# Six plain chunks instead of eight ahead of the pair runs of two feed-forward layers, with token-side sums in two bank sets and the plain chunks evacuated by ScalarE

## The chip, the cores and the metric

One core of a Trainium2 chip runs the whole model block. The metric is device time in microseconds, from three runs of the kernel before. TensorE multiplies, VectorE and GpSimd do elementwise work, ScalarE copies, squares and applies functions, SyncE issues the loads of the weights. SBUF holds 128 partitions; PSUM has eight banks of 128 x 512 floats, into which TensorE writes.

## The reference

Two transformer blocks over 512 tokens of width 1024. The change concerns the feed-forward layer of each, the first projection above all:

```
h = rms_norm(x, norm2_g[l])
f = jnp.square(jax.nn.relu(jnp.einsum('bsd,df->bsf', h, w_ff1[l])))
x = x + jnp.einsum('bsf,fd->bsd', f, w_ff2[l])
```

The second block has the same with `w_up`, `w_down` and `g_pre_mlp`. Width 1024 goes to 4096 and back. Ahead of the feed-forward layer stand, in block one, a gated unit with a convolution, and in block two, two kinds of attention.

## The kernel before, in words

All weights come as one stream of chunks of 128 x 1024, 512 KB each, into four slots. Each float is split into a high part (rounded to the 32-bit form that TensorE takes at full rate) and a low part (the rest), and each product is three: high times high, high times low, low times high. GpSimd splits the weights (`split_chunk`: one copy, `high`, and one subtraction, `low`, L564 and L567); ScalarE and VectorE split the activations (`xh`, `xl`). A chunk of the first projection gives one tile of 128 features x 512 tokens, by 8 x 3 = 24 products over 512 columns.

The feed-forward layer's hidden width of 32 tiles is done in two halves of 16 (`FH`). In each half the first projection is followed by the second one ("down"). The first half has `PLAIN` = 8 plain chunks and then a run of pairs; the other half is a run of eight pairs. **A pair** computes two tiles (2 x 2 blocks: two halves of the tokens, two halves of the features) by seven block products instead of eight, in the manner of Strassen and Winograd. Each block product is 12 products over 256 columns (`product`), so a pair has 84 of them, where two plain chunks have 48 over 512 columns. The seven need sums on both sides:

- Token side, once per layer: four sums of x blocks for each of four rounds k (`scaled_parts`, `t_sums`, `t_round`). ScalarE scales two parts into banks 4 and 5, VectorE makes four sums there (L2326), ScalarE rounds them into `t_high`, VectorE makes the low parts `t_low` (L2331).
- Weight side, once per pair: four sums of the raw weights in banks 6 and 7 by VectorE (`weight_sums_first` L2360 and L2362, `weight_sums_last` L2368 and L2369), rounded by ScalarE (`sum_round`, L1683), low parts by VectorE (`weight_rest`, L2377).

VectorE adds the seven products up: `first_corner` (L2385) adds the second to the first, and must be done before the seventh may be written, since they share a bank; `second_product`, `fifth_product` and so on follow. A finished tile goes through relu, square (`uh`, high) and low part (`rest_of_tile`, L2422).

The plain chunks of a layer feed TensorE while the token-side sums and the first pair's weight sums are made. Three of them run together while x is still being finished (`feed_first`, `several`); the others follow one by one, in banks `c % 4`. Behind the first products of the sixth chunk stand four turns (transposes) of the norm's summed squares (`norm_sums`), in bank 7 (`NB`). Tiles 0 to 3 are evacuated (relu, out of PSUM) by VectorE between the rounds of token sums, tiles 4 to 7 by ScalarE.

The order on each engine is that in which the code of its block is written; engines wait for each other by counting semaphores. The functions that the change touches are `plain_tiles` (ScalarE), `plain_run` and `t_sums` (VectorE), `feed_first` and `pair` (TensorE), `split_pair` (GpSimd). The projections, the attention and the second halves are not touched.

## Time and profile before

| | us |
|---|---|
| runs of before | 1082.06, 1082.08, 1083.15 (median 1082.08) |
| profiled execution | 1081.88 |
| its span | 1080.2 |
| TensorE busy | 1064.1, 99% of the span |
| VectorE busy | 701.3, 65% |
| GpSimd busy | 673.6, 62% |
| ScalarE busy | 400.7, 37% |
| end of the plain chunks, pairs: first layer | 193.1, 230.6 |
| end of the plain chunks, pairs: second layer | 791.85, 830.7 |

Busy time of TensorE is modelled: neighbouring products overlap in the pipeline, so how fast it goes is read from the starts. In the rows, a time in us from the span's start, a duration, the engine, the line, the operation and its operands stand in this order; [16.44 <-PE bank L766] is idle time just before and what ended it.

### The profile page before, as it was taken

What the parts mean: (1) busy time and instruction counts of PE and PEld (TensorE: products, weight loads), DVE (VectorE), ACT (ScalarE), POOL (GpSimd) and SP (SyncE); (2) the same over time, 40 slices, a digit from 0 to 9 for tenths busy, and PEclk for the clock granted to TensorE, in tenths of its full rate; (3) what the DMA queues carried; (4) which work ended last, traced back from release to release, by engine and by line L of the source; (5) the groups of instructions that cost most, each with busy time, mean ns of one, the idle gap of its engine ahead of it and who ended that gap; (6) DMA issues with size and microseconds to landing.
All of it is one profiled execution on the core that took longest, in us unless ns stands there. A gap on an engine that the chain in (4) does not pass through costs nothing.

```text
span 1080.2 us, 17261 instructions
## 1 busy us (share of the span) xinstructions
PE 1064.1 (99%) x6163; PEld 931.6 (86%) x6163; DVE 701.3 (65%) x1381; ACT 400.7 (37%) x817; POOL 673.6 (62%) x460
## 2 busy tenths in 40 slices
PE   9999999999999999999999999999999999999997
PEld 6878888998899988889788787777899888999886
DVE  5999778961158854548689878676888113886033
ACT  5156565540015541220202346655665000465012
POOL 7979857577636676667556433135856763557762
PEclk9999999999999999999999999999999999999999
DMA  7422223243213343334443232112223932234412
GB/s 262 137 91 66 61 96 98 80 155 117 97 59 118 111 156 104 100 110 142 117 133 102 90 86 60 40 60 78 61 96 134 198 98 66 92 118 173 179 59 78
DMA packets 52251, 115.54 MB, mean 107 GB/s; under 512 B 21840, under 2 KB 22480, under 8 KB 52176
## 3 DMA queue, kind: packets, MB, share of 16 engines
q1 hardware_dynamic: 31200, 105.40, 30.2%
q10 hardware_dynamic: 20976, 9.15, 3.4%
q8 instruction: 46, 0.75, 0.3%
q14 instruction: 29, 0.24, 0.1%
HBM read 105.09 MB, written 4.19 MB: 101 GB/s over the span
## 4 chain that ended last, share of the span: by engine, by line
PE 81%; DVE 11%; ACT 3%; issue 2%; POOL 2%; DMA 1%; SPq 0%; DVEq 0%; ACTq 0%; POOLq 0%
PE bank L766 80%; DVE bank L2118 5%; PE bank L1296 1%; POOL wl L567 1%; DVE tmp L2010 1%; ACT wh L1683 1%; DMA x<-xT 1%; DVE wl L2377 0%; DVE bank L2010 0%; POOL wh L564 0%; DVE gpad L2010 0%; DVE bank L2360 0%; PE bank L910 0%; ACT uh L1699 0%; DVE x L2191 0%
## 5 line engine op out<-in xcount | busy, mean ns | idle before, releaser
L567 POOL TENSOR_TENSOR wl<-raw,wh 128x1024 fp32r<-128x1024 f32 x140 | 334.2, 2387 | 11.7
L564 POOL TENSOR_SCALAR wh<-raw 128x1024 fp32r<-128x1024 f32 x139 | 149.2, 1073 | 231.7 <-PE bank L766 177.3
L766 PE MATMUL bank<-xh,wh 128*128 128x512 f32 (+2 forms) x747 | 256.4, 344 | 2.4 <-ACT vg L1577 1.5
L766 PE MATMUL bank<-xh,wl 128*128 128x512 f32 (+2 forms) x747 | 248.4, 336 | 0.0
L766 PE MATMUL bank<-xl,wh 128*128 128x512 f32 (+2 forms) x744 | 246.2, 338 | 0.8 <-DVE xl L2029 0.8
L766 PEld LDWEIGHTS bank<-xh,wh 128*128 128x128 f32 x747 | 141.9, 190 | 33.2 <-issue 19.5
L766 PEld LDWEIGHTS bank<-xl,wh 128*128 128x128 f32 x744 | 140.9, 190 | 14.2 <-DVE xl L2029 4.0
L766 PEld LDWEIGHTS bank<-xh,wl 128*128 128x128 f32 x747 | 142.0, 190 | 11.1
L1683 ACT ACTIVATE wh<-bank 128x512 fp32r<-128x512 f32 x96 | 52.2, 596 | 241.8 <-DVE bank L2362 103.1
L766 PE MATMUL bank<-uh,wh 128*128 128x512 f32 x320 | 123.2, 385 | 1.8 <-DVE ss L2412 0.9
L766 PE MATMUL bank<-uh,wl 128*128 128x512 f32 x320 | 121.3, 379 | 0.0
L766 PE MATMUL bank<-ul,wh 128*128 128x512 f32 x320 | 117.4, 379 | 0.0
L766 PE MATMUL bank<-t_high,wh 128*128 128x256 f32 x384 | 107.1, 279 | 0.3 <-DVE sq L2418 0.2
L766 PE MATMUL bank<-t_low,wh 128*128 128x256 f32 x384 | 105.6, 275 | 0.0
L766 PE MATMUL bank<-t_high,wl 128*128 128x256 f32 x384 | 105.6, 275 | 0.0
L766 PE MATMUL bank<-wh,uh 128*128 128x512 f32 x256 | 97.1, 379 | 0.4 <-POOL wl L567 0.4
L766 PE MATMUL bank<-wl,uh 128*128 128x512 f32 x256 | 97.0, 379 | 0.0
L766 PE MATMUL bank<-wh,ul 128*128 128x512 f32 x256 | 97.0, 379 | 0.0
L2377 DVE TENSOR_TENSOR wl<-bank,wh 128x512 fp32r<-128x512 f32 x96 | 63.2, 682 | 24.4 <-ACT wh L1683 24.1
L2010 DVE TENSOR_TENSOR bank<-bank,rb 128x512 f32<-128x512 f32 x16 | 11.2, 700 | 100.8 <-PE bank L766 100.8
L701 POOL TENSOR_SCALAR wh<-raw 128x512 fp32r<-128x512 f32 x24 | 15.0, 623 | 98.8 <-PE bank L766 98.8
L766 PEld LDWEIGHTS bank<-t_high,wh 128*128 128x128 f32 x384 | 73.6, 192 | 1.6 <-issue 0.6
(338 smaller groups left out, 2104.8 us busy)
## 6 DMA issues: line engine op xcount, KB each, us to landing
raw<-wstream SPq DMA_DIRECT2D x188, 512.0 KB, 3.5
x<-xT SPq DMA_DIRECT2D x8, 256.0 KB, 4.8
x4rows<-x_rows ACTq DMA_DIRECT2D x4, 512.0 KB, 7.5
out<-x4rows SPq DMA_DIRECT2D x8, 256.0 KB, 2.1
qd<-ropey ACTq DMA_DIRECT2D x16, 64.0 KB, 2.1
kd<-ropey ACTq DMA_DIRECT2D x16, 64.0 KB, 2.1
qa<-ropey SPq DMA_DIRECT2D x16, 64.0 KB, 2.0
ka<-ropey SPq DMA_DIRECT2D x16, 64.0 KB, 2.0
```

The lines of the kernel that those rows point to most:

```text
L564: nc.gpsimd.tensor_scalar(wh[c][:], raw[c][:], 1.0, 1.0, ALU.mult, ALU.mult).then_inc(high_ready, 1)
L567: nc.gpsimd.tensor_tensor(wl[c][:], raw[c][:], wh[c][:].bitcast(F32), ALU.subtract).then_inc(split_ready, 1)
L701: nc.gpsimd.tensor_scalar(high_b[:, 0:512], b[:, 512:], 1.0, 1.0, ALU.mult, ALU.mult).then_inc(high_ready, 1)
L766: return nc.tensor.matmul(out, stationary, moved, start=start, stop=stop)
L1296: last = nc.tensor.transpose(out[:, j * P:j * P + P], probs[2 * (n % 3) + e][:, j * P:j * P + P], ident[:])
L1683: A(wh[slot_of(p, role)][:, 512 * part:512 * part + 512], bank[7 - made % 2][:], ACT.Copy).then_inc(sum_rounded, 1)
L2010: return V.tensor_tensor(out, p, q, ALU.mult)
L2118: ins = V.scalar_tensor_tensor(out=out, in0=src, scalar=w, in1=acc, op0=ALU.mult, op1=ALU.add)
L2377: V.tensor_tensor(wl[slot][:, at], bank[7 - made % 2][:], wh[slot][:, at].bitcast(F32), ALU.subtract).then_inc(sum_ready, 1)
```

## The change

`PLAIN` goes from 8 to 6, so each layer has one pair more (five instead of four) behind its plain chunks. What makes room for that:

- The token sums of round k use banks 4 and 5 or banks 6 and 7 in turn (`t_banks`), and high and low parts of two sums lie in one tensor (`t_sides`), so that one operation over 512 columns rounds two sums, and one makes two low parts.
- All plain tiles are evacuated by ScalarE; VectorE has no evacuation left there.
- The turned squares go to bank 5 in the first layer and stay in bank 7 in the second (`norm_bank`), and wait for the token sums that used the bank.
- The first pair's slots, product banks and waits are numbered so that what follows stays as it was (`slot_of`, `free_at`, `FIRST_BANK`).
- On VectorE, the four small operations on the norm's rows stand behind the second layer's run of pairs instead of ahead of it.

```
-PLAIN = 8
+PLAIN = 6
...
+FIRST_BANK = (3, 0, 3, 1)
...
-    return (PAIR_RUNS[run_of(p)][0] + role) % SLOTS
+    first, _, count = PAIR_RUNS[run_of(p)]
+    return (first + 2 * count + role) % SLOTS
+
+
+def free_at(p, role):
+
+    first = PAIR_RUNS[run_of(p)][0]
+    return first - SLOTS + (slot_of(p, role) - first) % SLOTS + 1
...
+        t_sides = [at("t_sides0", [P, 2, 2, 4, Q], F32R, behind), at("t_sides1", [P, 2, 2, 4, Q], F32R, tmp_at)]
+        t_high = [t_sides[i // 2][:, i % 2, 0] for i in range(4)]
+        t_low = [t_sides[i // 2][:, i % 2, 1] for i in range(4)]
...
+        t_banks = [(bank[4], bank[5]), (bank[6], bank[7])] * 2 + [(bank[6], bank[7]), (bank[4], bank[5])] * 2
...
-            return bank[(7 * place_in(p) + i + run_of(p) // 3) % 5][:, EARLY]
+            return bank[(7 * place_in(p) + i + FIRST_BANK[run_of(p)]) % 5][:, EARLY]
+
+        def norm_bank(i):
+            return bank[5 if i == 5 else 7]
...
-                    pool.wait_ge(chunk_done, n - 3)
+                    pool.wait_ge(chunk_done, free_at(p, 0))
...
+                pe.wait_ge(t_ready, 14 if i == 13 else 6)
+                norm_sums(i, ss, 0, sq_added, squares)
...
-                    hooks = {0: lambda: norm_sums(i, ss, 0, sq_added, squares)} if c == 5 else {}
+                    hooks = {0: lambda: feed_norm(i, squares)} if c == PLAIN - 1 else {}
...
-                    pe.wait_ge(evacuated, e - 3)
+                    pe.wait_ge(evacuated, e - 2)
...
-                    pe.wait_ge(evacuated, e - 2)
+                    if run in (0, 2):
+                        pe.wait_ge(t_ready, 16 if run else 6)
...
-                    pe.wait_ge(t_ready, 32 if run else 16)
+                    pe.wait_ge(t_ready, 16 if run else 8)
...
+                if k % 4 >= 2:
+                    act.wait_ge(t_ready, 2 * k - 2)
+                for b, part, columns in zip(t_banks[k], (k % 4, 4 + k % 4), (EARLY, LATE)):
+                    A(b[:, EARLY], x[:, part, columns], ACT.Copy, scale=col(gain, part)).then_inc(scaled_part, 1)
...
-                for t, src in enumerate((bank[4][:, EARLY], bank[4][:, LATE], bank[5][:, EARLY], bank[5][:, LATE])):
-                    A(t_high[t][:, k % 4], src, ACT.Copy).then_inc(t_rounded, 1)
+                for sides, b in zip(t_sides, t_banks[k]):
+                    A(sides[:, :, 0, k % 4], two(b[:]), ACT.Copy).then_inc(t_rounded, 1)
...
+                def evacuate(c):
+                    act.wait_ge(chunk_done, c0 + c + 1)
+                    act.wait_ge(ul_ready, first + c - 1) if c >= 2 else act.wait_ge(sq_added, 6 * KT if first else 2 * KT)
+                    A(two(sq[c % 2][:]), by_token(bank[c % 4][:]), ACT.Relu).then_inc(evacuated, 1)
+
+                def squared(c):
                     act.wait_ge(evacuated, evacuations(first + c) + 1)
                     A(uh[:, c], sq[c % 2][:], ACT.Square).then_inc(uh_ready, 1)
                     A(sq[c % 2][:], sq[c % 2][:], ACT.Square).then_inc(square_ready, 1)
-                    if c < 3:
-                        scaled_parts(k0 + c + 1, gain)
-                    if c == PLAIN - 3:
-                        norm_sd(norm)
-                        sum_round(p, 0)
-                        sum_round(p, 1)
-                    if c == PLAIN - 2:
-                        sum_round(p, 2)
-                        sum_round(p, 3)
+
+                scaled_parts(k0, gain)
+                if first:
+                    act.wait_ge(xl_ready, 5 * KT)
+                else:
+                    act.wait_ge(xl_ready, 2 * KT)
+                    act.wait_ge(sq_added, 2 * KT)
+                scaled_parts(k0 + 1, gain)
+                t_round(k0)
+                evacuate(0)
+                t_round(k0 + 1)
+                scaled_parts(k0 + 2, gain)
+                squared(0)
+                evacuate(1)
+                scaled_parts(k0 + 3, gain)
+                t_round(k0 + 2)
+                squared(1)
+                evacuate(2)
+                t_round(k0 + 3)
+                squared(2)
+                evacuate(3)
+                squared(3)
+                evacuate(4)
+                squared(4)
+                norm_sd(norm)
+                sum_round(p, 0)
+                sum_round(p, 1)
+                evacuate(5)
+                squared(5)
+                sum_round(p, 2)
+                sum_round(p, 3)
...
+                def t_rest(i):
+                    dve.wait_ge(t_rounded, 2 * k + i + 1)
+                    sides = t_sides[i]
+                    V.tensor_tensor(sides[:, :, 1, k % 4], two(t_banks[k][i][:]),
+                                    sides[:, :, 0, k % 4].bitcast(F32), ALU.subtract).then_inc(t_ready, 1)
...
-                for c in range(4):
-                    t_sums(k0 + c, 0, gain)
-                    if c == 0:
-                        dve.wait_ge(sq_added, (6 if norm == 13 else 2) * KT)
-                    evacuate(c)
-                    t_sums(k0 + c, 1, gain)
-                    if c < 3:
-                        rest(c)
+                t_sums(k0, 0, gain)
+                t_sums(k0 + 1, 0, gain)
+                t_sums(k0, 1, gain)
+                t_sums(k0 + 1, 1, gain)
+                t_sums(k0 + 2, 0, gain)
+                rest(0)
+                t_sums(k0 + 2, 1, gain)
+                t_sums(k0 + 3, 0, gain)
+                rest(1)
+                t_sums(k0 + 3, 1, gain)
+                rest(2)
+                norm_total(norm)
+                dve.wait_ge(t_ready, 2 * k0 + 8)
+                weight_sums_first(p)
                 rest(3)
-                rest(4)
-                norm_total(norm)
-                weight_sums_first(p)
-                rest(5)
                 weight_rest(p, 0)
                 weight_rest(p, 1)
+                weight_sums_last(p)
+                rest(4)
                 norm_factor(norm)
-                weight_sums_last(p)
-                rest(6)
                 weight_rest(p, 2)
                 weight_rest(p, 3)
-                rest(7)
+                rest(5)
...
+            pair_run(2)
             dve.wait_ge(rn_ready, 14)
             link(mul(row_scale[:], rn[:, 0:TB], rn[:, 0:TB]))
             link(mul(row_weight[:], row_scale[:], row_scale[:]))
             link(V.reciprocal(row_weight[:], row_weight[:]))
             V.tensor_scalar(row_weight_mean[:], row_weight[:], 1.0 / D, None, ALU.mult).then_inc(row_scaled, 1)
-            pair_run(2)
```

Two places show what moves. ScalarE, first layer, from the rounding of the second round of token sums on; before (sq_75 and sq_76 are the two buffers of tiles, t_high_139 to 142 the high parts of the four token sums):

```order
L1673 ACTIVATE t_high_139<-bank 128x256
L1673 ACTIVATE t_high_140<-bank 128x256
L1673 ACTIVATE t_high_141<-bank 128x256
L1673 ACTIVATE t_high_142<-bank 128x256
L1717 ACTIVATE uh<-sq_76 128x512
L1718 ACTIVATE sq_76<-sq_76 128x512
L1664 ACTIVATE bank<-x,cols 128x256
L1666 ACTIVATE bank<-x,cols 128x256
```

and now, from the same point (t_sides_139 and 140 hold two sums each; L1727 is the evacuation):

```order
L1688 ACTIVATE t_sides_139<-bank 128x2x256
L1688 ACTIVATE t_sides_140<-bank 128x2x256
L1682 ACTIVATE bank<-x,cols 128x256 x2
L1731 ACTIVATE uh<-sq_75 128x512
L1732 ACTIVATE sq_75<-sq_75 128x512
L1727 ACTIVATE sq_76<-bank 128x512
L1682 ACTIVATE bank<-x,cols 128x256 x2
L1688 ACTIVATE t_sides_139<-bank 128x2x256
L1688 ACTIVATE t_sides_140<-bank 128x2x256
L1731 ACTIVATE uh<-sq_76 128x512
L1732 ACTIVATE sq_76<-sq_76 128x512
```

ScalarE has two evacuations between the rounds, and each rounding is two operations instead of four. VectorE, first layer, from the last addition to the sum of squares on; before (L2326 are the token sums, L2436 the evacuation, L2331 the low parts of the sums, L2422 that of a tile):

```order
L2309 TENSOR_TENSOR ss<-sq_76,bank 128x512
L2326 SCALAR_TENSOR_TENSOR bank<-x,cols,bank 128x256 x4
L2436 TENSOR_SCALAR sq_75<-bank 128x512
L2331 TENSOR_TENSOR t_low_143<-bank,t_high_139 128x256
L2331 TENSOR_TENSOR t_low_144<-bank,t_high_140 128x256
L2331 TENSOR_TENSOR t_low_145<-bank,t_high_141 128x256
L2331 TENSOR_TENSOR t_low_146<-bank,t_high_142 128x256
L2422 TENSOR_TENSOR ul<-sq_75,uh 128x512
L2326 SCALAR_TENSOR_TENSOR bank<-x,cols,bank 128x256 x4
```

and now:

```order
L2362 SCALAR_TENSOR_TENSOR bank<-x,cols,bank 128x256 x8
L2368 TENSOR_TENSOR t_sides_139<-bank,t_sides_139 128x2x256
L2368 TENSOR_TENSOR t_sides_140<-bank,t_sides_140 128x2x256
L2368 TENSOR_TENSOR t_sides_139<-bank,t_sides_139 128x2x256
L2368 TENSOR_TENSOR t_sides_140<-bank,t_sides_140 128x2x256
L2362 SCALAR_TENSOR_TENSOR bank<-x,cols,bank 128x256 x4
L2457 TENSOR_TENSOR ul<-sq_75,uh 128x512
L2368 TENSOR_TENSOR t_sides_139<-bank,t_sides_139 128x2x256
L2368 TENSOR_TENSOR t_sides_140<-bank,t_sides_140 128x2x256
L2362 SCALAR_TENSOR_TENSOR bank<-x,cols,bank 128x256 x4
```

VectorE makes the sums of two rounds at once, and has no evacuation; the low parts are two operations a round. From the norm's totals on (the first pair's weight sums, three low parts of tiles and the weight sums' low parts) its order is that of before, with tiles 3, 4 and 5 in the place of 5, 6 and 7; only the reciprocal of the norm stands two sums and a low part later.

## Rows read from the trace of the kernel before

**Rows 1.** The page, part 1: busy time, share, instructions.

```profile
PE 1064.1 (99%) x6163; PEld 931.6 (86%) x6163; DVE 701.3 (65%) x1381; ACT 400.7 (37%) x817; POOL 673.6 (62%) x460
```

**Rows 2.** TensorE in order of time, first layer.

```profile
166.78 0.38 PE L766 MATMUL bank<-xh,wh 128*128 128x512 f32 x1
...
177.57 0.38 PE L766 MATMUL bank<-xh,wl 128*128 128x512 f32 x1
...
178.15 0.46 PE L766 MATMUL bank<-xh,wh 128*128 128x512 f32 x1
...
193.12 0.27 PE L766 MATMUL bank<-xh,wh 128*128 128x256 f32 x1
...
230.53 0.28 PE L766 MATMUL bank<-t_high,wl 128*128 128x256 f32 x1
```

**Rows 3.** TensorE in order of time, second layer.

```profile
765.51 0.38 PE L766 MATMUL bank<-xh,wh 128*128 128x512 f32 x1
...
791.85 0.27 PE L766 MATMUL bank<-xh,wh 128*128 128x256 f32 x1
...
799.78 0.28 PE L766 MATMUL bank<-xh,wl 128*128 128x256 f32 x1
...
800.09 0.35 PE L766 MATMUL bank<-t_high,wh 128*128 128x256 f32 x1
...
801.75 0.35 PE L766 MATMUL bank<-xh,wh 128*128 128x256 f32 x1
...
830.63 0.28 PE L766 MATMUL bank<-t_high,wl 128*128 128x256 f32 x1
```

**Rows 4.** VectorE in order of time, the first addition of a pair.

```profile
197.63 0.41 DVE L2385 TENSOR_TENSOR sq<-bank,first_product 128x256 f32<-128x256 f32 x1
...
228.25 0.41 DVE L2385 TENSOR_TENSOR ss<-bank,first_product 128x256 f32<-128x256 f32 x1
...
799.52 0.42 DVE L2385 TENSOR_TENSOR sq<-bank,first_product 128x256 f32<-128x256 f32 x1
...
808.90 0.41 DVE L2385 TENSOR_TENSOR ss<-bank,first_product 128x256 f32<-128x256 f32 x1
...
828.46 0.41 DVE L2385 TENSOR_TENSOR ss<-bank,first_product 128x256 f32<-128x256 f32 x1
```

**Rows 5.** VectorE in order of time, second layer.

```profile
766.01 1.80 DVE L2326 SCALAR_TENSOR_TENSOR bank<-x,cols,bank 128x256 f32<-128x256 f32 x4 [2.39 <-ACT bank L1666]
...
797.74 1.23 DVE L2010 TENSOR_TENSOR row_scale<-rn 128x4 f32<-128x4 f32 x1
...
868.58 0.69 DVE L2878 COPY x<-bank 128x512 f32<-128x512 f32 x1 [16.44 <-PE bank L766]
```

**Rows 6.** VectorE in order of time, first layer, plain chunks.

```profile
163.59 1.79 DVE L2326 SCALAR_TENSOR_TENSOR bank<-x,cols,bank 128x256 f32<-128x256 f32 x4
...
166.62 0.69 DVE L2436 TENSOR_SCALAR sq<-bank 128x512 f32<-128x512 f32 x1 [1.25 <-PE bank L766]
...
167.23 1.41 DVE L2331 TENSOR_TENSOR t_low<-bank,t_high 128x256 fp32r<-128x256 f32 x4
...
168.56 2.22 DVE L2422 TENSOR_TENSOR ul<-sq,uh 128x512 fp32r<-128x512 f32 x1
...
185.97 0.69 DVE L2422 TENSOR_TENSOR ul<-sq,uh 128x512 fp32r<-128x512 f32 x1 [0.17 <-ACT sq L1718]
```

**Rows 7.** ScalarE in order of time, both layers.

```profile
187.51 0.58 ACT L1715 ACTIVATE sq<-bank 128x512 f32<-128x512 f32 x1
...
765.12 0.46 ACT L1664 ACTIVATE bank<-x,cols 128x256 f32<-128x256 f32 x1
```

**Rows 8.** GpSimd in order of time, first layer.

```profile
167.85 2.38 POOL L567 TENSOR_TENSOR wl<-raw,wh 128x1024 fp32r<-128x1024 f32 x1
...
182.93 1.28 POOL L696 TENSOR_TENSOR wl<-raw,wh 128x512 fp32r<-128x512 f32 x1
...
193.45 0.62 POOL L701 TENSOR_SCALAR wh<-raw 128x512 fp32r<-128x512 f32 x1 [7.98 <-PE bank L766]
```

51 lines of the change are left out of this document (13 added, 38 removed).

## The prediction

> **What bounds the kernel now.** The page comes first: TensorE is busy for 99% of the span [rows 1], and its granted clock is full in all 40 slices, so the question is where its stream of products gets shorter, and where a wait is put into it. The profiled execution took 1081.88 us, 0.20 below the median of the runs. Its span is 1080.2, so 1.7 us lie around it, and I add 0.2 at the end to come to the median.
>
> TensorE's own row in order of time is next, by starts, since the printed durations of neighbours overlap. In the first section chunk 3 starts at 166.78 and the first pair at 193.12 [rows 2]. That is 26.34 us for five chunks of 24 products and four turns of the norm. The turns and the slower step behind them take 0.42 (the products on either side of the turns, at 177.57 and 178.15, start 0.58 apart, 0.36 more than one product needs, and the next step is 0.07 longer), so a product over 512 columns takes (26.34 - 0.42) / 120 = 0.216 us, a chunk 5.18. The four pairs begin at 193.12, and their last product starts at 230.53: 335 steps, 0.1117 us for 256 columns, 9.38 a pair. TensorE had no gap anywhere in these 336 products.
>
> In the second section it had. The pairs ran from 791.85 to 830.74, 38.89 us instead of 37.53 [rows 3]. From the last product of one group at 799.78 to the first two groups later at 801.75 are 13 steps, 1.45 us of work, and they took 1.97: two waits of 0.52 together, one of them ahead of the product at 800.09, with the slower step of 0.07 behind the first, and one behind the second; 0.6 in all. The other 0.8 come in small gaps of the later pairs.
>
> Why they come is seen on VectorE. Once per pair it adds TensorE's second product to the first (line 2385). These additions start at 799.52, 808.90 and, two pairs on, 828.46 in the second section [rows 4]: 9.38 after the first pair, then 9.78 each. TensorE needs only 9.38, so as soon as VectorE has no lead, **a pair costs 9.78, not 9.38**. In the first section the same addition starts 4.5 us behind the pair's own start (197.63 against 193.12), and the fourth at 228.25 [rows 4]. VectorE falls back there too, by 10.2 a pair, from 4.5 us to 228.25 - (193.12 + 3 x 9.38) = 7.0 behind, and it spends a lead that the plain chunks gave it. In the second section it is at 7.7 from the start, and there the products wait. So the lead in front of the first pair is what hides the pairs' slower engine. The last addition is followed by 2.28 us to the end of the last product (828.46 to 830.74) where VectorE sets the pace.
>
> **What the change takes away.** Per section two plain chunks go, 48 x 0.216 = 10.36 us, and 84 products of 256 columns come, 9.38: 0.98 less, 1.96 in both, if TensorE never waits. The 0.6 of waits between 799.78 and 801.75 go too: VectorE was late with the addition at 799.52 because four small operations on the norm's rows, 797.74 to 799.52 [rows 5], stood ahead of it. They now stand behind the last pair, where VectorE next waits 16.44 us for TensorE [rows 5], so they cost nothing there. The upper limit of the gain is 2.6 us.
>
> The Trainium skill speaks against the change here: "TensorE: Matmul & The Clock Gate", section "Back-to-back issue gap", gives about 81 ns for products of 128 columns and about 131 for 512 in a sustained stream. By that a 256-column product is about 98 ns (an estimate, linear between the two), a pair 84 x 98 = 8.2 us against 6.3 for two chunks, and the change would cost 1.9 per section. This trace has 216 and 112 ns.
>
> **What comes 10.4 us earlier.** The first pair starts at 182.7 instead of 193.12. What it needs must be made in ten microseconds less:
>
> - VectorE loses four evacuations and two low parts ahead of the pair, each about 0.6 of its time (the evacuation at 166.62 and what follows it start 0.61 apart [rows 6]). The 16 small low parts of the turned sums become 8 wide ones, 1.20 for what took 1.33 per round. That is 4 x 0.6 + 2 x 0.6 + 0.5 = 4.1 us, not 10.4. So its lead shrinks by about 6.
> - ScalarE takes the evacuations: 4 x 0.55 by the one that it has already, 0.58 at 187.51 [rows 7]. It is busy for 37% of the span against VectorE's 65%, and laid out it stays ahead of VectorE in the first section. The tightest of them is the evacuation of tile 1, needed by chunk 5: about 170.7 against 177.1 in the first section, 773.3 against 775.9 in the second. No wait.
> - GpSimd's split of the pair's first chunk now waits for chunk 4 (177.1 + 0.33, the lag of GpSimd's copy at 193.45 behind the chunk that ended at 193.12) and takes 1.1 + 2 x 1.25 and about 0.8 of waits for the port [rows 8]: 182.0 against 182.7. A margin of 0.7; it would be the next to be late. The DMA loads of the four following chunks wait for splits as before and have some 5 us to spare.
> - ScalarE's copies of the weight sums need the slot of chunk 5, which ends with the plain part (182.7 + 0.33).
>
> **The port.** A low part of a plain tile reads sq and uh, both in SBUF. At 168.56 it took 2.22 us and at 185.97 0.69 [rows 6]. In the first case GpSimd was inside its own 2.38 us subtraction (167.85 to 170.23), and VectorE's ended 0.6 after that [rows 8]. So such an operation waits for the end of GpSimd's instruction. Operations that read PSUM and one SBUF operand are not held. The Trainium skill says so too ("SBUF — State Buffer", section "🔬 SBUF: two separate sides": the shared pair is an exclusive lock for the whole instruction); by it the evacuations taken off VectorE never waited, and the waits all stay with what is left. The trace agrees: the evacuation at 166.62 took 0.69.
>
> **First section, laid out.** Chunk 5 ends at 182.7. Products 0 and 1 of the pair follow. The copies of the first two sums can run from 183.0 and their low parts on VectorE stand at 183.7 to 184.9; product 2 is due at 185.4: no wait. The other sums take 1.2, to 186.2. Then a low part of a tile meets GpSimd's copy of a whole chunk (about 1.1, twice the 0.62 of half a chunk less its start; it begins 0.33 after product 1, 185.7 to 186.8) and ends at 187.4, and the third sum's low part at 188.1, where product 4 is due at 188.05. With 0.23 us from VectorE to TensorE (the addition at 799.52 and 0.34 of its time, to the product at 800.09) and the 0.07 of a restart it is 0.3 late. Another low part wants 188.7, meets GpSimd's subtraction and ends at 190.2. So the first addition is at 190.2, 7.5 behind the pair's start, as in the second section of before. From there: 190.2 + 9.38 + 3 x 9.78 + 2.28 = 231.2. Before, the run ended at 230.64. **The section is 0.55 us longer**, where TensorE's own time would make it 0.98 shorter. Without the two meetings at the port (1.0 and 0.5) the addition is at 188.7, and TensorE's own 182.7 + 46.9 + 0.1 = 229.7 binds: 0.9 shorter. With one more meeting of a full 1.28 it is 1.8 longer.
>
> **Second section.** The turned sums start at 766.01 on VectorE, because ScalarE comes to them at 765.12 only [rows 5, 7], while chunk 3 starts at 765.51. Set against chunk 3, that is 3.7 us later than in the first section (766.01 - 765.51 = 0.5 against 163.59 - 166.78 = -3.2). VectorE has 15.3 us of work from there to the second weight sum (four rounds of sums at 1.70, eight low parts, three low parts of tiles and the totals at 0.6, two weight sums 1.3), and about 1.4 of waits for ScalarE and the port: 782.7. The copy on ScalarE, behind its squares, is at 783.5 to 783.9, the low part ends at 784.7 (785.1 if the tile's low part ahead of it meets GpSimd), and product 2 is due at 784.1: 0.9 late (0.3 to 1.3). Product 4 then waits 0.8 more (to 1.5). TensorE's own sum is 781.45 + 46.9 + 1.7 = 830.05; VectorE's is 789.5 (790.5) + 41.0 = 830.5 (831.5). Before: 830.74. I take 830.65, a gain of 0.1, with -1.2 (no meeting, product 2 only 0.3 late) and +0.8 as ends.
>
> **Sum.** 1081.88 + 0.55 - 0.1 = 1082.3; against the median 1082.5. All else (the projections, the attention, runs 1 and 3) is the same code and the same row of instructions.
>
> **The rivals.**
>
> 1. *TensorE alone counts* (chance 0.13). The waits at the port fall between the low parts, and the sections come out at -0.9 and -1.2: 1081.88 - 2.1 + 0.2 = 1080.0. For it: VectorE is lighter by 4.1 us and ScalarE has room. Against: VectorE's pace of 9.78 and 10.2 in the two sections [rows 4], and 6 us less lead.
> 2. *Slower: the first sums of the second section are late by whole instructions of GpSimd* (0.10). Place: the low part at 782.8 and that at 786.6. If each meets a subtraction of 1.28 from its start, 1.3 is added (my sum has half of each), and if the pairs behind go at the first section's 10.2 [rows 4] in all four intervals, 1.7: 1085.5. It decides from 2.2 us over the median. Against: a meeting costs what is left of GpSimd's instruction, half of it on average.
> 3. *The plain part starves* (0.04): a chunk waits for ScalarE's evacuation, or the pair for GpSimd's split (margin 0.7). A late split of one more port wait of 1.28 in each section: 0.6 x 2, 1083.7.
> 4. *Short products cost more than the rows' 0.1117* (0.01): if each of the pair's seven groups began with the slower step of 0.07 that stands behind a wait, 7 x 0.07 x 2 = 1.0: 1083.5. The 336 steps of the first section speak against it [rows 2]. The rule on the issue gap, named above, is of this kind.
> 5. *My forecast, the gain given back by VectorE's pace* (0.72): 1081.3 to 1083.7.
>
> **The numbers.** A measurement of this kernel tells about 0.2%, 2.2 us, from no change: faster means under 1079.9, slower over 1084.2. Of rival 1 about half is under 1079.9 when the ends of both sections add up: 0.06. Of 2 most is over 1084.2, of 5 very little: 0.10. The rest, 0.84, is within. The range reaches from 1080.9 (into rival 1) to 1084.0 (through rival 3).
>
> **What would show it.** In the changed kernel: the first products of 256 columns at about 182.7 and 781.4; the first addition at about 190.2 and 789.5 to 790.5; 9.78 between the additions from the second on, in the first section too; no wait of TensorE for product 2 in the first section, but one in the second; waits of low parts for GpSimd inside the plain part; the end of the pairs at 231.2 and 830.7. My forecast is wrong if TensorE's five pairs take 46.9 us in the first section (rival 1), or if the second section ends past 832 (rival 2).

## The result, and the profile after

The changed kernel takes 1086.16 us (median of 17 executions, 1083.42 to 1093.0) against 1081.86 (17 executions, 1081.4 to 1083.15): a ratio of 1.0056, 95% interval 1.0043 to 1.0068. It is slower by 4.3 us in the median and by 6.0 in the mean (1087.9 against 1081.9), and its time is spread as that of the kernel before is not: six executions lie at 1083.4 to 1084.3, four at 1085.5 to 1088.0, seven at 1091.5 to 1093.0. The profiled one took 1091.5. I had forecast 1082.5, range 1080.9 to 1084.0.

The page of the changed kernel, part 1, beside [rows 1]:

```profile
span 1089.7 us, 17403 instructions
PE 1066.2 (98%) x6235; PEld 935.1 (86%) x6235; DVE 716.2 (66%) x1387; ACT 409.2 (38%) x819; POOL 670.1 (61%) x462
```

TensorE is busy 2.1 us longer in a span that is 9.5 us longer: the rest is waiting. The same functions have other line numbers now (products L775 for L766, first additions L2420 for L2385, low parts of tiles L2457 for L2422). In order of time, the first layer on VectorE and TensorE, beside [rows 2, 4]:

```profile
190.08 0.41 DVE L2420 TENSOR_TENSOR sq<-bank,first_product 128x256 f32<-128x256 f32 x1
...
228.78 0.41 DVE L2420 TENSOR_TENSOR sq<-bank,first_product 128x256 f32<-128x256 f32 x1
```

```profile
231.06 0.38 PE L775 MATMUL bank<-uh,wh 128*128 128x512 f32 x1
```

The first addition was forecast at 190.2, the end of the pairs at 231.2; they are at 190.08 and 231.06. Between the first addition and the fifth are 38.70 us, 9.37 and then 9.77 to 9.78 each, and nothing waited for product 2. The pairs end 0.42 us later than before (230.64). Set against chunk 3, which starts at 166.67 here and at 166.78 before, the section is 0.53 us longer (I had 0.55). TensorE stays 0.40 to 0.48 late up to 530 us. In the second layer TensorE:

```profile
792.93 0.28 PE L775 MATMUL bank<-xh,wl 128*128 128x256 f32 x1
794.12 0.46 PE L775 MATMUL bank<-t_sides,wh 128*128 128x256 f32 x2 [0.91 <-issue]
...
796.76 0.28 PE L775 MATMUL bank<-t_sides,wl 128*128 128x256 f32 x1
798.28 0.49 PE L775 MATMUL bank<-t_sides,wh 128*128 128x256 f32 x2 [1.25 <-DVE wl L2412]
...
840.34 0.38 PE L775 MATMUL bank<-wh,uh 128*128 128x512 f32 x1
```

The step from 792.93 to 794.12 is 1.08 us longer than the 0.11 of a product (product 2 is late), that from 796.76 to 798.28 1.41 longer (product 4). VectorE and GpSimd around it:

```profile
791.68 1.74 DVE L2457 TENSOR_TENSOR ul<-sq,uh 128x512 fp32r<-128x512 f32 x1
793.34 1.28 DVE L2412 TENSOR_TENSOR wl<-bank,wh 128x512 fp32r<-128x512 f32 x2
...
795.86 1.71 DVE L2457 TENSOR_TENSOR ul<-sq,uh 128x512 fp32r<-128x512 f32 x1
...
797.58 1.25 DVE L2412 TENSOR_TENSOR wl<-bank,wh 128x512 fp32r<-128x512 f32 x2
...
799.35 0.41 DVE L2420 TENSOR_TENSOR sq<-bank,first_product 128x256 f32<-128x256 f32 x1
```

```profile
791.58 1.28 POOL L715 TENSOR_TENSOR wl<-raw,wh 128x512 fp32r<-128x512 f32 x1
...
795.74 1.27 POOL L708 TENSOR_TENSOR wl<-raw,wh 128x512 fp32r<-128x512 f32 x1
```

Both low parts meet a subtraction of GpSimd just after its start and take 1.7 instead of the 0.69 of [rows 6]. I had charged half a meeting each. From chunk 3 (774.39) to the end of the pairs (840.34) are 65.95 us, against 830.74 - 765.51 = 65.23 before: +0.72, where I had -0.1.

Together that is +1.14 of the 9.5 us. The other 8.4 lie between 535 and 564 us, in the attention stage, whose code is unchanged. TensorE is 0.48 late at 530 us, 1.52 from 537 on, behind a wait for ScalarE, and 8.86 from 564 on, behind a wait that ends at 559.67; then it stays there. ScalarE at the entry of the stage, before and after (eight DMA issues that move rotated queries into qd, called the burst below, then copies of scores):

```profile
513.71 5.00 ACTq L1780 DMA_DIRECT2D qd<-ropey  x8
518.82 0.66 ACT L1800 ACTIVATE sq<-bank 128x256 f32<-128x256 f32 x2 [6.78 <-issue]
```

```profile
514.19 6.49 ACTq L1815 DMA_DIRECT2D qd<-ropey  x8
...
517.94 2.10 ACTq L1815 DMA_DIRECT2D qd<-ropey  x1
...
520.78 0.66 ACT L1835 ACTIVATE sq<-bank 128x256 f32<-128x256 f32 x2 [8.81 <-issue]
```

The second row is one of the eight by itself: seven issues take 0.5 to 0.6 us, that at 517.94 takes 2.10. The DMA queues from 518 to 520 us in the changed kernel show what else happens. The profile calls the traffic of q8 and q14 "instruction": a transfer there is a fetch of some engine's program.

```profile
q10 hardware_dynamic: 93, 0.12, 24.5%
q8 instruction: 1, 0.02, 5.0%
```

Before, q8 moves nothing from 518 to 520 us; its fetch is in the microsecond from 525 on:

```profile
q8 instruction: 1, 0.02, 8.5%
```

Then VectorE and GpSimd, before:

```profile
521.52 0.29 DVE L2603 TENSOR_TENSOR work<-work,mask 128x128 f32<-128x128 f32 x1
```

```profile
522.06 1.05 POOL L564 TENSOR_SCALAR wh<-raw 128x1024 fp32r<-128x1024 f32 x1 [2.95 <-PE bank L766]
523.19 2.38 POOL L567 TENSOR_TENSOR wl<-raw,wh 128x1024 fp32r<-128x1024 f32 x1
```

and in the changed kernel:

```profile
522.97 1.07 DVE L2631 SCALAR_TENSOR_TENSOR work<-tmp,wnat,work 128x256 f32<-128x256 f32 x1
524.07 2.34 DVE L2636 TENSOR_TENSOR work<-work,mask 128x128 f32<-128x128 f32 x1
...
530.91 2.52 DVE L2628 TENSOR_SCALAR work<-sq,wnat 128x384 f32<-128x384 f32 x1
...
536.66 3.70 DVE L2631 SCALAR_TENSOR_TENSOR work<-sq,wnat,work 128x384 f32<-128x384 f32 x2 [1.06 <-ACT sq L1835]
```

```profile
523.85 2.41 POOL L578 TENSOR_TENSOR wl<-raw,wh 128x1024 fp32r<-128x1024 f32 x1
...
530.53 2.68 POOL L578 TENSOR_TENSOR wl<-raw,wh 128x1024 fp32r<-128x1024 f32 x1
```

The mask addition began 1.67 us ahead of GpSimd's subtraction (its low split) before, and ahead of the copy too. Now it begins 0.22 behind the subtraction's start and ends with it, and the next subtractions are met as well. TensorE waits until 559.67, and the granted clock falls; the stretches 480 to 560 and 560 to 600 us, before and after (length, busy time of PE, PEld, DVE, ACT and POOL, then the mean granted clock, 1.00 being the level of 2.4 GHz, the DMA share and GB/s):

```profile
480.00:560.00 80.00, 79.91 (x408) 66.73 (x408) 58.50 (x93) 13.33 (x31) 49.04 (x28) 1.00 0.44 129
560.00:600.00 40.00, 39.99 (x189) 33.82 (x188) 39.86 (x127) 7.36 (x16) 25.81 (x16) 1.00 0.33 109
```

```profile
480.00:560.00 80.00, 73.95 (x377) 61.25 (x376) 60.92 (x75) 13.65 (x31) 46.84 (x26) 0.98 0.42 125
560.00:600.00 40.00, 40.00 (x179) 34.75 (x179) 39.90 (x120) 4.81 (x7) 23.96 (x14) 0.96 0.29 92
```

```profile
559.67 0.80 PE L775 MATMUL bank<-wh,xh 128*128 128x512 f32 x1 [5.37 <-DVE tmb L2045]
```

The wait costs TensorE 5.5 us, start to start. The clock was granted at its lower level (1.2 GHz, 0.50 in the rows) from 556.3 to 563.2 us, from 2 us after TensorE's last product to 3.5 us behind the wait, and that costs the other 1.8 of the 7.3:

```profile
556.00:559.60 3.60, 0.00 (x0) 0.00 (x0) 3.32 (x7) 0.00 (x0) 0.00 (x0) 0.55 0.41 146
559.60:563.20 3.60, 3.53 (x8) 2.85 (x9) 3.50 (x8) 0.00 (x0) 0.00 (x0) 0.51 0.00 0
```

### The profile page after: what moved, and what is told of

The parts are those of the page before. It is cut to its first block, busy times and chain, and to the rows that moved or that the text cites. A ratio compares the mean times of both kernels' runs of the same rounds, so it can differ in the third digit from the quotient of the medians.

```text
span 1089.7 us, 17403 instructions
## 1 busy us (share of the span) xinstructions
PE 1066.2 (98%) x6235; PEld 935.1 (86%) x6235; DVE 716.2 (66%) x1387; ACT 409.2 (38%) x819; POOL 670.1 (61%) x462
## 4 chain that ended last, share of the span: by engine, by line
PE 77%; DVE 14%; ACT 3%; issue 3%; POOL 2%; ACTq 1%; DMA 0%; DVEq 0%; SPq 0%; POOLq 0%
PE bank L775 75%; DVE bank L2153 5%; DVE work L2631 1%; ACTq L1815 1%; PE bank L1313 1%; DVE tmp L2045 1%; POOL wl L578 1%; DVE bank L2045 1%; DVE xl L2064 1%; DVE bank L2362 0%; DMA x<-xT 0%; POOL wh L575 0%; DVE ropey L2607 0%; DVE gpad L2045 0%; PE bank L921 0%
## 5 line engine op out<-in xcount | busy, mean ns | idle before, releaser
L578 POOL TENSOR_TENSOR wl<-raw,wh 128x1024 fp32r<-128x1024 f32 x136 | 325.0, 2390 | 11.4
L575 POOL TENSOR_SCALAR wh<-raw 128x1024 fp32r<-128x1024 f32 x135 | 144.3, 1069 | 239.8 <-PE bank L775 182.4
L775 PE MATMUL bank<-xh,wh 128*128 128x512 f32 (+2 forms) x739 | 251.3, 340 | 2.7 <-ACT vg L1594 1.5
L775 PE MATMUL bank<-xh,wl 128*128 128x512 f32 (+2 forms) x739 | 243.1, 332 | 0.0
L775 PE MATMUL bank<-xl,wh 128*128 128x512 f32 (+2 forms) x736 | 240.6, 334 | 0.2 <-DVE xl L2064 0.2
L775 PEld LDWEIGHTS bank<-xh,wh 128*128 128x128 f32 x739 | 140.6, 190 | 32.7 <-issue 19.5
L775 PEld LDWEIGHTS bank<-xl,wh 128*128 128x128 f32 x736 | 139.6, 190 | 12.8 <-DVE xl L2064 3.4
L775 PEld LDWEIGHTS bank<-xh,wl 128*128 128x128 f32 x739 | 140.7, 190 | 10.2
L775 PE MATMUL bank<-t_sides,wh 128*128 128x256 f32 x832 | 145.1, 278 | 2.2 <-DVE wl L2412 1.2
L775 PEld LDWEIGHTS bank<-t_sides,wh 128*128 128x128 f32 x832 | 126.1, 192 | 4.1 <-DVE wl L2412 1.4
L775 PE MATMUL bank<-uh,wh 128*128 128x512 f32 x320 | 123.2, 385 | 1.7 <-DVE ss L2447 0.9
L775 PE MATMUL bank<-uh,wl 128*128 128x512 f32 x320 | 121.3, 379 | 0.0
L775 PE MATMUL bank<-ul,wh 128*128 128x512 f32 x320 | 117.4, 379 | 0.0
L775 PE MATMUL bank<-t_sides,wl 128*128 128x256 f32 x416 | 114.4, 275 | 0.0
L775 PE MATMUL bank<-wh,uh 128*128 128x512 f32 x256 | 97.1, 379 | 0.4 <-POOL wl L578 0.4
L775 PE MATMUL bank<-wl,uh 128*128 128x512 f32 x256 | 97.0, 379 | 0.0
L775 PE MATMUL bank<-wh,ul 128*128 128x512 f32 x256 | 97.0, 379 | 0.0
L2412 DVE TENSOR_TENSOR wl<-bank,wh 128x512 fp32r<-128x512 f32 x104 | 68.6, 683 | 25.7 <-ACT wh L1698 25.7
L775 PEld LDWEIGHTS bank<-t_sides,wl 128*128 128x128 f32 x416 | 79.9, 192 | 0.0
```

The lines of the kernel that those rows point to most:

```text
L575: nc.gpsimd.tensor_scalar(wh[c][:], raw[c][:], 1.0, 1.0, ALU.mult, ALU.mult).then_inc(high_ready, 1)
L578: nc.gpsimd.tensor_tensor(wl[c][:], raw[c][:], wh[c][:].bitcast(F32), ALU.subtract).then_inc(split_ready, 1)
L775: return nc.tensor.matmul(out, stationary, moved, start=start, stop=stop)
L2412: V.tensor_tensor(wl[slot][:, at], bank[7 - made % 2][:], wh[slot][:, at].bitcast(F32), ALU.subtract).then_inc(sum_ready, 1)
```

## The experiments

"Waits" below are instructions that wait for a semaphore raised long ago: they lengthen an engine's program and do next to nothing. Each kernel is compared with the kernel before on the same chip (medians 1081.74 to 1082.05).

**Which engine's fetch, and is it lateness?** Four kernels. `b_pad9`, `b_pad4` and `a_pad9` add waits on ScalarE behind the first layer's pairs (to the kernel before, and to the changed one); `b_late` adds products in the first down projection.

```diff
             pair_tiles(1)
+            for _ in range(18):             # 9 instructions; 8 for 4 in b_pad4
+                act.wait_ge(x_loaded[0], 16)
```

```diff
+                    if c0 == C_FF1 and h == 0 and c == 2:
+                        for _ in range(2):
+                            mm(bank[5][:], wh[(dn0 + c) % SLOTS][:, 0:P], uh[:, 0], start=True, stop=True)
                     chunk_transposed((dn0 + c) % SLOTS, bank[4 + o][:], uh, ul, tiles0=8 * kk,
```

> The kernel before, with nine more semaphore instructions on ScalarE behind the pairs of the first layer, for semaphores that have long been raised, so that each later instruction of ScalarE stands as far from the start of its program as in the changed kernel (the first move of qd at place 461 in both). Nothing of the feed-forward change is in it. Theory 1 (an instruction fetch of ScalarE falls into its burst of eight DMA issues, and the attention stage falls behind from there): one issue of that burst takes about 2.1 us in place of 0.61, the relu behind it starts 1.5 late, and the time becomes that of the changed kernel less its two feed-forward sections: 1083 to 1092, median near 1085, with a wide spread. Theory 2 (the attention stage falls behind since everything arrives 0.42 us later): 1082 as before, and no long issue. Theory 3 (all of the loss lies in the two feed-forward sections): 1082.

1081.88 (1081.6 to 1083.91), ratio 1.0002 (0.9993 to 1.0011); no long issue. Theory 1 falls.

> The kernel before with four more semaphore instructions on ScalarE instead of nine: the place at which the changed kernel's long issue lay is then between two bursts, where ScalarE waits for products. Theory 1: as the kernel before, 1082, no long issue. That any extra instruction there costs: part of the loss of the nine, 1083 to 1085. Theories 2 and 3: 1082.

1081.82 (1081.56 to 1082.14), 0.9998 (0.9989 to 1.0007).

> The changed kernel, with nine more semaphore instructions on ScalarE at the same place, which moves the place of the fetch out of the burst of issues and into a stretch in which ScalarE waits. Theory 1: no long issue; before's time and the two feed-forward sections' +1.1 to +1.5: 1083.0 to 1083.9, with a spread as narrow as before's. Theory 2: no change against the changed kernel, 1083 to 1093 with a median near 1086. Theory 3: as theory 2.

1085.62 (1083.76 to 1093.49), 1.0054 (1.0033 to 1.0075). The spread stays, and the long issue too (1.51 us, at 518.88), beside a fetch on q8 at 519. What moved with ScalarE's program was the fetch on q14. So q8 belongs to another engine. Its fetches are 20 to 29 us apart (481, 501, 525, 554, 581 and 607 us before), and TensorE is the engine that goes through so many instructions; in the changed kernel it has 76 more ahead of this stage.

> The kernel before, with two extra 512-column products on TensorE in the down projection of the first layer, written into a bank that the next product clears: everything behind arrives 0.43 us later, as in the changed kernel (+0.42), and no other engine has an instruction more or fewer. Theory 1: 1082.5, narrow. Theory 2: as the changed kernel, 1083 to 1092 with a median near 1085. Theory 3: 1082.5.

1082.17 (1081.79 to 1082.66), 1.0001 (0.9992 to 1.001). Only 0.08 us of the delay were left at 480 us, so this says nothing; `b_later` has the delay nearer to the stage. Theory 3 needs no run: 8.4 of the 9.5 us lie outside the two sections.

**TensorE's program.** `b_pe77` and `a_pe65` put waits between the products of the first layer.

```diff
                 for k in range(8):
+                    if padding:             # filled ahead of feed_first(C_FF1, ...)
+                        for _ in range(padding.pop()):
+                            pe.wait_ge(split_ready, 1)
```

> The kernel before, with 77 more instructions on TensorE between the plain chunks and the down projection of the first layer, all of them waits for a semaphore that has long been raised. The changed kernel has 76 more there (36 products of two instructions each, and some waits), since a pair takes more products than two plain chunks. In the traces so far the fetch on queue q8 comes at 525 us before and at 518 to 519 in the changed kernel and in it with ScalarE padded, at the very issue of a move of qd that takes 2.1 or 1.5 us in place of 0.61; padding ScalarE by nine moved the fetch on q14 (511 to 508), not this one. Theory 4 (q8 carries TensorE's instructions; the longer TensorE program brings its fetch into ScalarE's burst of DMA issues at 514 to 519 us, and the attention stage falls behind): the fetch at 517 to 519, a long issue, and 1083 to 1092 in place of 1082, with a median near 1084 to 1085. Theory 5 (the loss comes with something else of the changed code, as VectorE's or SyncE's program or the buffers of the sections): 1082, narrow, with or without a moved fetch. Waits that cost TensorE time themselves would show as gaps in the first layer, up to 2 us.

1082.71 (1081.63 to 1091.62), 1.0029 (1.001 to 1.0049). Four of twelve executions at 1085.2, 1090.1, 1091.2 and 1091.6: with nothing of the feed-forward change in it. The profiled execution, at 1081.85, is not one of them. In it the fetch on q8 is at 518, and the eighth issue takes 1.31:

```profile
518.26 1.31 ACTq L1786 DMA_DIRECT2D qd<-ropey  x1
```

> The changed kernel with 65 more waits on TensorE at the same place, which by the rate of the traces (77 instructions for some 7 us) brings the fetch from 518 to about 512 us, ahead of the burst that begins at 514.2. Theory 4: no long issue, 1083.1 to 1083.9, narrow, plus what the waits cost by themselves. Theory 5: 1083 to 1093 with a median near 1086, as the changed kernel.

1084.72 (1083.83 to 1092.91), 1.0057 (1.0034 to 1.0079): a miss. The profiled execution has the fetch at 512 and no long issue, but four of ten took 1091.65 or more.

> The changed kernel with 180 more waits on TensorE in the first layer, so that its program is 256 instructions longer than before's at the attention stage (5284 against 5028 at its first product with qi), 256 being by the traces about one fetch on q8 (27 us apart, with some 9.3 to 11 instructions of TensorE per us). The fetches then lie at 524 and 552 us, as before. Theory 4 in its full form: no execution at 1091, and 1083.3 to 1084.2, narrow, apart from what the waits cost by themselves. If executions of 1091 remain, the place of the fetch is not what separates the kernels, as the run with 65 waits (fetch at 512, no long issue, four of ten executions at 1091.7 or more) already makes one doubt; then the lateness of 0.77 us there and the first layer's code stay as causes.

1083.57 (1083.23 to 1085.35), 1.0018 (1.001 to 1.0027), nothing near 1091; two of eleven at 1085.3. The fetch is back at 525, the burst back at 5.00 us. A program 256 instructions longer than before's at this place (76 + 180) has this fetch where before's is; one 76 or 141 longer does not. Theory 5 falls. TensorE's wait of 5.37 us has shrunk but not gone:

```profile
550.85 1.10 DVE L2642 TENSOR_TENSOR work<-work,mask 128x128 f32<-128x128 f32 x1
```

```profile
553.33 0.48 PE L775 MATMUL bank<-wh,xh 128*128 128x512 f32 x1 [0.17 <-DVE tmb L2051]
```

This mask addition begins 0.08 us behind the start of a copy of GpSimd (550.77, 1.04 long) and lasts to its end. In the kernel before it stood at 550.12, ahead of the copy (550.39), took 0.29, and TensorE didn't wait. Here TensorE loses 0.44 us.

**One layer at a time.** Same code as in the changed kernel in one layer, as before in the other (PLAIN, banks and evacuations chosen by layer).

```diff
+PLAIN1, PLAIN2 = 6, 8                       # layer1_only; 8, 6 in layer2_only
-PAIR_RUNS = ((C_FF1 + PLAIN, PLAIN, FH // 2 - PLAIN // 2), ...
+PAIR_RUNS = ((C_FF1 + PLAIN1, PLAIN1, FH // 2 - PLAIN1 // 2), ...
```

> The change in the first layer alone; the second layer as in the kernel before (eight plain chunks, row operations ahead of its pairs). TensorE's program has 76 instructions more ahead of the attention stage, as in the changed kernel. By theory 4 (the fetch of TensorE's instructions on q8 falls at 518 us into the burst of moves, and VectorE and GpSimd then fall behind in the attention stage in part of the executions): lowest run 1082.0 to 1082.6 (the section's +0.4 and what a long issue costs by itself), several executions at 1085 to 1091, median 1083 to 1085. If the attention stage is not hurt by the first layer's change (theory 5, and by the second layer's own code): 1082.3, narrow.

1091.26 (1083.62 to 1092.62), 1.0061 (1.0038 to 1.0083). The profiled execution (1092.22) repeats the pattern: an issue of 1.90 at 517.82, the fetch at 517, the mask addition 2.35 long.

> The change in the second layer alone, the row operations behind the pairs in it. No instruction ahead of the attention stage differs from the kernel before. Theory 4: no execution at 1085 or more; before's 1081.8 and the second section's +0.7: 1082.5, and narrow. Theory 5 with the second layer's buffers or code as its cause: the wide spread of the changed kernel.

1082.89 (1082.35 to 1084.7), 1.0012 (1.0003 to 1.0021), narrow. It costs 1.15, where the section showed 0.72 in the changed kernel.

> The kernel before with four extra products of a chunk of qi ahead of that chunk's own (its bank is cleared by the chunk), some 0.65 us of TensorE at 483 us: the attention stage begins later against nothing else of its own; the fetch of TensorE's instructions is moved by less than 1 us against the burst. This mends the run with the delay in the first layer's down projection, of whose 0.43 us only 0.08 were left at 480 us. If lateness of TensorE alone brings the attention stage into trouble (theory 2): 1083 to 1092 with a wide spread. Theory 4: 1082.0 to 1082.7, narrow.

The edit is four products into the bank of the chunk C_QI ahead of its own. 1081.97 (1081.76 to 1083.02), 1.0 (0.9991 to 1.0009), although in the profiled execution (1083.02, the longest) TensorE ran 1.19 us late through the whole stage. 0.85 of that stood before the edit, from the start of the execution on. Theory 2 falls: the burst (514.90) and GpSimd's low split (524.37) are 1.2 late as well, so the engines shift together.

**The row operations.** In `b_rows_late` the four row operations are the only thing moved; in `a_rows_early` they are moved back.

```diff
+            pair_run(2)
             dve.wait_ge(rn_ready, 14)
             link(mul(row_scale[:], rn[:, 0:TB], rn[:, 0:TB]))
...
-            pair_run(2)
```

> The kernel before with one part of the change alone: the four row operations of the second layer's norm stand behind its pairs on VectorE. If they are free where they go and cost where they stood: TensorE's waits in the second section, 0.45 us in all, go, and the time is 1081.5 to 1082.0, which can't be told from 1081.9. If the sections have other causes of waiting: 1081.9.

1080.64 (1080.4 to 1081.04), 0.999 (0.9981 to 0.9999): 1.15 us faster than before, more than the 0.45 of visible waits. The first addition is at 797.95, the last at 827.62, against 799.52 and 828.46 [rows 4]: an addition made earlier moves the end where VectorE sets the pace. It is the fastest kernel here.

> The changed kernel with that part undone: the four row operations ahead of the pairs of the second layer, 1.9 us of VectorE. If the row operations are what my step on the second section needs: the first addition 1.9 later, product 4 of the first pair as much later, and 1.5 to 1.9 more than the changed kernel, lowest run 1085 in place of 1083.4. If VectorE has slack there: the lowest run at 1083.4 to 1083.9. The spread of the changed kernel stays by all theories, since nothing ahead of the attention stage changes.

1084.77 (1084.39 to 1087.04, five executions). The lowest is 1.0 above the changed kernel's, and the pairs take 50.58 us from their first product to the start of their last, against 49.86: 0.7, not 1.9. Two of the five executions are at 1087.0; neither is the profiled one.

**Is it ScalarE's lateness?** `b_hold15` and `b_hold07` put copies ahead of the seventh move, with no fetch moved.

```diff
+                        if dst is qd and m == 0 and (hh, part) == (3, 0):
+                            for i in range(3):      # 2 of 256 columns in b_hold07
+                                A(va[:, i, 0:420], cosr[:, 0:420], ACT.Relu)
```

> The kernel before, with ScalarE held up for about 1.4 to 1.5 us ahead of the seventh of the eight moves in its first burst to qd: three copies of 420 columns into a tile that is written later. That is the excess of the long issue in the changed kernel (2.10 less 0.61), without a moved fetch. Theory 4a (it is ScalarE's lateness behind the burst that brings the attention stage out of step: VectorE's score products start late and meet GpSimd's split): relu at 520.3 in place of 518.8, the mask addition at 523.0 or later, executions at 1088 to 1092 in most runs. Theory 4b (the fetch does its harm in some other way, the long issue is only its sign): 1082 to 1083.5, narrow.

1081.93 (1081.62 to 1082.44), 1.0 (0.9991 to 1.0009). The copies didn't hold the issues. In order of time:

```profile
513.45 3.72 ACTq L1783 DMA_DIRECT2D qd<-ropey  x6
517.22 0.55 ACT L1782 ACTIVATE va<-cosr 128x420 f32<-128x420 f32 x1 [5.78 <-issue]
517.30 0.52 ACTq L1783 DMA_DIRECT2D qd<-ropey  x1
517.68 0.54 ACT L1782 ACTIVATE va<-cosr 128x420 f32<-128x420 f32 x1
517.85 0.61 ACTq L1783 DMA_DIRECT2D qd<-ropey  x1
518.13 0.54 ACT L1782 ACTIVATE va<-cosr 128x420 f32<-128x420 f32 x1
518.57 0.65 ACT L1803 ACTIVATE sq<-bank 128x256 f32<-128x256 f32 x2
```

The seventh issue starts 0.08 behind the first copy, the copies run beside it, and the copy of scores behind the burst stands 5.12 us behind the burst's start, as before (5.11).

> As the run with the long hold, with two copies of 256 columns, some 0.6 us: about the excess of the shorter long issues (1.28 to 1.31 less 0.61) of profiled executions that ended at 1081.85 and 1084.39 and stayed in step. Theory 4a with a threshold: 1082 to 1082.6, narrow. Without one (each bit of lateness costs): 1083 to 1086. Theory 4b: 1082.

1082.03 (1081.73 to 1082.55). Neither run says anything on the question.

> The changed kernel with 68 more waits on TensorE, next to the run with 65, to look again at what remained open there: its profiled execution had no long issue and ended at 1083.83, but four of its ten ended at 1091.7 or more. Theory 4 expects in a profiled execution above 1090 a long issue on ScalarE or another engine beside a fetch at 512 to 513 us or at 537 us, since the fetch is not at the same distance from the burst in each execution. If such an execution shows no long issue anywhere, there is a second way into the slow course.

1088.4 (1083.72 to 1092.35, six executions). Here the fetch, with 68 waits, is at 517 and an issue at 517.10 takes 1.28, where the run with 65 had it at 512. So the place of the fetch against the burst isn't the same in each execution, which may explain the miss of `a_pe65`; it isn't shown, since no execution of that kernel above 1090 has been profiled. This execution, 1085.4, shows something else. TensorE's lateness grows by 1.7 us between 480 and 490 us, ahead of the burst. The granted clock is at the lower level for 3.4 us there. TensorE isn't idle; just before, from 480.6 to 482.4 us, it has 16 products of a single column, as in the kernel before, where the clock stays at 1.00:

```profile
482.70:486.10 3.40, 3.40 (x12) 3.40 (x11) 1.24 (x5) 1.94 (x4) 1.13 (x1) 0.50 0.13 40
```

Without it this execution would be at 1083.7, with the two lowest.

Issues can't be passed by ScalarE's copies, so the last three kernels hold it with further issues:

```diff
+                        if dst is qd and m == 0 and (hh, part) == (3, 0):
+                            for i in range(2):      # 1, 2, 3
+                                act.dma_start(spare[i], mask[0:32, 0:384]).then_inc(spared, 16)
```

> The kernel before with one more DMA issue on ScalarE ahead of the seventh move of the first burst to qd (32 rows of 384 numbers of a constant, to a place that nobody reads); no fetch is moved. In the two runs with copies in this place ScalarE's relu was not late, since its copies run beside its issues; an issue can't be passed. By the profiled executions so far, VectorE's mask addition in this stage starts 1.67 us ahead of GpSimd's low split where the burst takes 5.00 us, 0.95 to 1.00 ahead (and takes 1.01 to 1.05 in place of 0.29) where it takes 5.68 to 5.91, and 0.22 behind it (and takes 2.34) where it takes 6.30 to 6.49; only those last end above 1090. Theory 4a: with a burst of 5.64 the addition is about 1.0 ahead and the time 1081.9 to 1082.7. Theory 4b (the fetch harms in another way): 1081.9.

1081.88 (1081.62 to 1082.29), 0.9997 (0.9988 to 1.0007).

> With two more issues: a burst of 6.28 us, at the edge. Theory 4a: the addition meets the split in part of the executions, 1082 to 1091. Theory 4b: 1081.9 to 1082.3.

1090.53 (1090.01 to 1092.01, four executions), 1.0081 (1.0064 to 1.0098).

> With three more issues: a burst of 6.92 us. Theory 4a: the addition starts behind the split's start in each execution and takes over 2 us, TensorE waits 5 us at 553 us, its granted clock falls, and all executions lie at 1088 to 1093, with no fetch moved. Theory 4b: 1082 to 1083.

1090.81 (1090.14 to 1091.34, four executions), 1.008 (1.0063 to 1.0096).

One DMA issue more costs nothing, two cost 8.5 us in the median, and none of their four executions is under 1090.0. The added issues also move data of their own, 48 KB each; no run has that alone. `b_issue2`, VectorE, GpSimd and the stretches, where the pattern of the changed kernel stands with the fetch at 525, its old place:

```profile
523.06 2.34 DVE L2608 TENSOR_TENSOR work<-work,mask 128x128 f32<-128x128 f32 x1
...
530.08 2.52 DVE L2600 TENSOR_SCALAR work<-sq,wnat 128x384 f32<-128x384 f32 x1
```

```profile
522.84 2.41 POOL L569 TENSOR_TENSOR wl<-raw,wh 128x1024 fp32r<-128x1024 f32 x1
```

```profile
480.00:560.00 80.00, 74.03 (x374) 61.46 (x375) 62.12 (x76) 13.67 (x31) 46.11 (x26) 0.97 0.42 123
560.00:600.00 40.00, 40.00 (x183) 34.56 (x183) 39.76 (x119) 5.01 (x8) 23.97 (x15) 0.97 0.31 95
```

The profiled executions, from the first issue of the burst to the end of the eighth move, and the start of the mask addition against GpSimd's low split:

| kernel | burst, us | addition against split, its length | time, us |
|---|---|---|---|
| before, b_pad4, b_pad9, b_late, b_later, a_pe65, a_pe180, b_rows_late, layer2_only, b_hold15, b_hold07 | 5.00 to 5.02 | 1.65 to 1.67 ahead, 0.29 | 1081.04 to 1083.83 |
| b_issue1 | 5.55 | 1.11 ahead, 1.17 | 1081.85 |
| a_rows_early, a_pe68, a_pad9, b_pe77 | 5.68 to 5.91 | 0.95 to 1.00 ahead, 1.01 to 1.05 | 1081.85 to 1085.4 |
| b_issue2 | 6.04 | 0.22 behind, 2.34 | 1090.01 |
| layer1_only, after | 6.30, 6.49 | 0.22 behind, 2.34 to 2.35 | 1092.22, 1091.5 |
| b_issue3 | 6.68 | an operation earlier, 0.29 behind, 2.41 | 1090.55 |

The lengths between 1.01 and 1.17 are the meeting with the copy again: in `b_issue1` the addition begins at 522.05, GpSimd's copy at 522.04, and both end by 523.2, ahead of the subtraction. That costs TensorE nothing here; a start behind the subtraction's does.

## Why the prediction was wrong

**Where it failed.** The step is the sentence on "all else (the projections, the attention, runs 1 and 3)" being "the same code and the same row of instructions", at 0 us. The code is the same, but it stands elsewhere in TensorE's program. A plain chunk is 24 products, a pair 84, so the first layer's change adds 36 products, with their weight loads and some waits 76 instructions. That brings a fetch of TensorE's instructions from 525 to 518 us, into ScalarE's burst of eight DMA issues, one of which then takes 1.3 to 2.1 us (shown: `b_pe77` makes it, `a_pe180` unmakes it). In the profiled executions up to a burst of 5.91 us at most 1 us follows, at the wait of 553. From 6.04 us on, VectorE's next operation on SBUF begins behind the start of GpSimd's subtraction instead of ahead of it and is held to its end, and one meeting leads to the next: a wait of 1.0 us at 536, one of 5.5 until 559.67, 1.8 for 3.5 us at the lower clock level, 8 to 9 us in all (shown: `b_issue1` to `b_issue3`, no fetch moved). That the changed kernel's extra falls on either side of that edge, and that this makes its spread, is argued: one execution of it has been profiled, and the shorter bursts are from its neighbours (`a_pad9`, `a_rows_early`, `b_pe77`). The fetch takes 2.5 of the 4.3 us of the median, since 1.8 stay with the fetch back in place (`a_pe180`), and 4.1 of the 6.0 of the mean.

The four executions between 1085.5 and 1088.0 seem to be something else. Their mean granted clock is 0.996 to 0.997, where the six lowest have 0.999 or 0.998. The 1085.4 of `a_pe68`, with 0.997, lost 1.7 us by one spell at the lower level. The two of `a_pe180` at 1085.3 have 0.997 too. The clock doesn't account for all of them: the two of `a_rows_early` at 1087.0 have 0.999. None but that of `a_pe68` has been profiled, so this stays open.

**First section:** right by its steps. Pairs at 182.65 (182.7), first addition at 190.08 (190.2), 9.78 a pair, no wait for product 2, the section +0.53 (+0.55). The gain of 0.98 on TensorE was given back by VectorE's pace as laid out.

**Second section:** the mechanism right, its size wrong. Product 2 was 1.08 late (I had 0.9, up to 1.3), product 4 another 1.41 (0.8, up to 1.5), the first addition 8.98 behind the pairs' start; the term came out at +0.72 in place of -0.1, inside the end of +0.8 that I gave. Both low parts met GpSimd at its instruction's start, which is rival 2 at its place, with 0.8 of its 3.0 us. "They cost nothing there" holds for the row operations, and they were worth more than the 0.6 that I gave them: alone they bring 1.15 (`b_rows_late`). So six plain chunks by themselves cost the second layer more than its +0.72: `layer2_only` is 1082.89 against 1080.64 with the row operations late and eight chunks, the one 1.15 above the kernel before, the other 1.15 below it.

**Sum.** 1083.57 (`a_pe180`) less 1081.74 is 1.8. Of it 1.2 are the two sections, and 0.44 the wait at 553 us, again a term of "all else" that I had at nothing: all four other kernels with the first layer's change whose profiled execution ended below 1086 (`a_pe65`, `a_pe68`, `a_pad9`, `a_rows_early`) meet the copy there too and lose 0.43 to 0.95. `b_later`, 1.19 us late, doesn't, so lateness alone isn't it, and no experiment takes it apart. The remaining 0.1 is within the noise. By these terms the forecast would have been about 1083.6, inside the range that I gave, and the fetch puts 2.5 on it. Rivals 1, 3 and 4 didn't happen: TensorE's five pairs were not at 46.9 us, no chunk waited for an evacuation, and products of 256 columns stayed at 0.11.

## What to carry to other kernels

An edit that changes how many instructions an engine has moves every later fetch of its program; look at where the instruction queues' transfers fall before and after, and which engine issues DMAs there. Before trusting that untouched stages stay at zero, ask how near they are to an edge: here 1 us of ScalarE's lateness decided on 8.5 us, while a shift of all engines by 1.2 us cost nothing. And test each part of a bundle alone: moving four small operations brought 1.15 us (1080.64), and six plain chunks lost in both layers (+0.53 in the first section, 2.25 in the second by `layer2_only` against `b_rows_late`).
